# Small tables issued later, token diagonals and squares made sooner, in the start of a one-core transformer step

## The chip, the cores and the metric

The kernel runs on one core of a Trainium2 chip. The core has a matrix engine (TensorE, PE in the profile), three engines for elementwise work (VectorE or DVE, ScalarE or ACT, GpSimd or POOL), a fifth that only issues transfers here (SyncE, SP), and 16 DMA engines that all issuers share. The metric is the time of one execution on the device in microseconds. Three executions of the kernel before took 838.27, 839.02 and 839.62 us; the median is 839.02 us.

## The reference

One layer of a hybrid backbone is applied to 512 latent tokens and 128 context tokens of width 1024: an adaptive RMS norm, one input projection, two kinds of linear attention, an output projection, and a mixture of 32 experts. The change lies ahead of the input projection, so only this part matters:

```python
def rmsnorm(x, w):
    y = xf * lax.rsqrt(jnp.mean(xf * xf, axis=-1, keepdims=True) + EPS)
    return (y * w.astype(jnp.float32)).astype(x.dtype)

mod = (jax.nn.silu(cond) @ w_ada + b_ada)[:, None, :]      # w_ada: 1024 x 6144
sh1, sc1, g1, sh2, sc2, g2 = jnp.split(mod, 6, axis=-1)
h = rmsnorm(x, norm1_w) * (1 + sc1) + sh1
proj = h @ w_in                                            # w_in: 1024 x 3616
```

There are two conditioning vectors, one for the latent tokens and one for the context tokens. The gate biases, gate matrices, head norms and retention decays are small inputs that are used after `proj`.

## The kernel before, in words

The 640 tokens are five tiles of 128 rows (`X[:, t, :]`, 512 KB each). The input projection needs them with the channels on the partitions, so each tile is turned, and the turn also applies the root of the norm: for tile t, TensorE multiplies each of eight 128x128 pieces of X by a diagonal matrix `diag[t]` whose entries are the 128 roots of the tile's rows. Four turned pieces fill one bank of PSUM, so a tile fills two banks, called the half 0 and the half 1 of a turned tile (job `("xT", t, half)`, line 1574). ACT moves half 0 to `hT`, DVE moves half 1 (`turned_half`, lines 806 to 809 and 1039 to 1042). These moves are called evictions below.

A diagonal is made in a chain over three engines, each step on the one before: ACT sums the squares of the tile's rows (line 813), DVE turns the sum into a mean square (step `("ms0", t)`, helper line 1035), POOL takes the root with a power of -0.5 (step `("rs0", t)`, `root`, line 653), and DVE multiplies the identity by the roots (step `("diag", t)`, line 1057).

The modulation needs `w_ada`. Its columns for the shift (m = 0) and the scale (m = 1) come as eight loads of 1 MB, `("ada", m, i)`, each of which is used by one chunk of four matmuls (`chunk(m, i)`, line 1554). SP issues all weight loads through a ring of four slots (line 523): load n waits until load n-4 has been used. The chunks of m = 0 sum in a bank that DVE copies at line 1062, those of m = 1 in another, copied at line 1069. Both sums are then brought onto partitions by eight small matmuls (`("mT", m)`, line 1585). Only when `mT` 1 has been read (lines 1047 and 1072, step `mcol`) are the turned tokens scaled and shifted (lines 825 and 1080), and the first matmul of the input projection (line 1634) waits for the first of these.

The order of TensorE's work in this start is the list `START` (lines 114 and 115). Banks are given out in that order, seven in turn, and a matmul that starts a bank waits until its last content has been evicted. Each of the other engines runs its own list in program order; it waits in place for what it needs. ACT issues the loads of the conditioning vectors, of the constants and of the five token tiles; POOL issues the small tables.

The consumers of the small tables are these: the biases and the norm of line 629 and 630 feed the matmul at line 1566 (`bT`); the columns `gbias`, `nw` and `lg` (semaphore `s_cols`) are waited for by ACT ahead of line 828 and by DVE at line 1123; `wgate` (`s_gate`) by TensorE at line 1642; `brow` and `wrow` (`s_mrow`) much later, in the modulation rows after the attention scores.

Of the kernel before, what the change touches and what calls it, by code (L numbers as in the profile page):

```python
# [7 lines left out]
KC = D // P  # L8
# [97 lines left out]
def turn(t):  # L106
    return [("xT", t, half) for half in range(2)]


def chunk(m, i):  # L110
    return [("ada", m, i)]


START = chunk(0, 0) + chunk(0, 1) + chunk(0, 2) + chunk(0, 3) + [("bT",)] + turn(0) + chunk(1, 0) + turn(1) + [("mT", 0)]
START += turn(2) + chunk(1, 1) + turn(3) + chunk(1, 2) + turn(4) + chunk(1, 3) + [("mT", 1)]


def plan_loads():
# [61 lines left out]
def build(nc, inp, outs):  # L180
# [10 lines left out]
    with ExitStack() as ctx:  # L191
# [176 lines left out]
        def is_filled(eng, job):  # L368
            b, turn = where(job)
            eng.wait_ge(filled[b], turn + 1)  # L370
# [24 lines left out]
        dve_order = []  # L395
        for t in range(TILES):
            dve_order += [("ms0", t), ("diag", t)]
            if t == 2:
                dve_order += ["mcol0"]
        dve_order += ["mr1", "mcol"] + [("hT", k, part) for part in ("lat", "ctx") for k in range(0, KC, 2)]  # L400
        act_order = ["cS", "cS32"] + [("ss", t) for t in range(TILES)]
        act_order += [("hT", k, part) for part in ("lat", "ctx") for k in range(1, KC, 2)] + ["lg", "softplus"]
        pool_order = ["cS32"] + [("rs0", t) for t in range(TILES)]
# [216 lines left out]
        def _(pool):  # L620
            chain = [0]

            def link(ins):
                chain[0] += 1
                ins.then_inc(pool_chain, 1)
                pool.wait_ge(pool_chain, chain[0])

            pool_done(nc.gpsimd.memset(cS32, 0.0), "cS32")
            pool.dma_start(modr[0:2 * KC, :], b_ada[0, 0:2 * D].rearrange("(k p) -> k p", p=P)).then_inc(s_row, 16)
            pool.dma_start(modr[2 * KC:3 * KC, :], norm1_w[0].rearrange("(k p) -> k p", p=P)).then_inc(s_row, 16)  # L630
            with nc.allow_non_contiguous_dma(reason="small columns"):
                for d, v in enumerate((ggbf, ggbb)):
                    pool.dma_start(gbias[:, d, :], v[0].rearrange("(g p) -> p g", p=P)).then_inc(s_cols, 16)
                for d, v in enumerate((ret_norm_w, gla_norm_w)):
                    pool.dma_start(nw[:, 4 * d:4 * d + 4], v[0].rearrange("(h p) -> p h", p=P)).then_inc(s_cols, 16)
# [2 lines left out]
            link(nc.gpsimd.memset(wgate, 0.0))  # L638
            for d, v in enumerate((ggwf, ggwb)):
                pool.dma_start(wgate[RANK * d:RANK * (d + 1), d, :], v[0]).then_inc(s_gate, 16)  # L640
            link(nc.gpsimd.memset(power, -0.5))
            link(nc.gpsimd.memset(ones_c, 1.0))

            link(nc.gpsimd.memset(wrow, 1.0))
            for cond in range(2):
                r0 = cond * 32
                pool.dma_start(brow[r0:r0 + 32, :], b_ada[0, 2 * D:6 * D].rearrange("(c n) -> c n", n=P)).then_inc(s_mrow, 16)
                pool.dma_start(wrow[r0 + 16:r0 + 24, :], norm2_w[0].rearrange("(c n) -> c n", n=P)).then_inc(s_mrow, 16)

            def root(ap, key, rkey):  # L650

                dve.wait(pool, key)
                pool_done(nc.gpsimd.tensor_tensor(ap, ap, power[:, 0:ap.shape[1]], ALU.pow), rkey)  # L653

            for t in range(TILES):
                root(rstd[:, t:t + 1], ("ms0", t), ("rs0", t))


            is_filled(pool, ("xT", CTX, 1))
            for n, (dst, c0) in enumerate(((rel[0], R_RELF), (rel[1], R_RELB), (tft[0], R_TF), (tft[1], R_TB))):  # L660
                pool.dma_start(dst, rconsts[:, c0:c0 + dst.shape[1]]).then_inc(s_rc, 16)

            def level_exponents(n):

# [119 lines left out]
        def _(sc):  # L784
# [21 lines left out]
            def turned_half(t):  # L806
                job = ("xT", t, 0)
                is_filled(sc, job)
                drains(f(hT[:, 0:4, t * P:(t + 1) * P], bk(job)[:, :].rearrange("p (k t) -> p k t", k=4), ACT.Copy), job)

            for t in range(TILES):
                sc.wait_ge(s_x[t], 16)
                act.done(f(xn[:, t, :], X[:, t, :], ACT.Square, accum_out=ss[:, t:t + 1]), ("ss", t))
                if t:
                    turned_half(t - 1)
            turned_half(CTX)
            sc.dma_start(tail[:, 0:2048], consts[:, C_ROT:C_ONES]).then_inc(s_tail, 16)
            sc.dma_start(ones_s, consts[:, C_ONES:C_ONES + P]).then_inc(s_tail, 16)
            for t in range(TILES):
# [203 lines left out]
        def _(dv):  # L1023
# [27 lines left out]
            for t in range(TILES):  # L1051
                act.wait(dv, ("ss", t))
                dve.done(mean_square(rstd[:, t:t + 1], ss[:, t:t + 1], D), ("ms0", t))
                if t:
                    turned_half(t - 1)
                pool_s.wait(dv, ("rs0", t))
                dve.done(v.tensor_scalar(diag[t], ident[:, :], rstd[:, t:t + 1], None, ALU.mult), ("diag", t))
                if t == 1:
                    is_filled(dv, ("bT",))
                    drains(v.tensor_copy(bn.rearrange("p m k -> p (m k)"), bk(("bT",))[:, 0:3 * KC]), ("bT",))  # L1060
                    is_filled(dv, ("mr",))
                    drains(v.tensor_copy(first_mod_rows[0], bk(("mr",))[:, :]), ("mr",))
                if t == 2:
                    is_drained(dv, ("bT",))
                    modulation(0)
                    dve.done(v.memset(st3[:, 0:1], 0.0), "mcol0")
            turned_half(CTX)
            dv.wait_ge(scale_summed, 1)
            dve.done(v.tensor_copy(first_mod_rows[1], mod_ps[:, :]), "mr1")
            modulation(1)  # L1070
# [906 lines left out]
```

## Time and profile before

| what | value |
|---|---|
| median of three executions | 839.02 us (838.27 to 839.62) |
| the profiled execution | 835.24 us |
| its span | 833.5 us |
| TensorE busy | 723.8 us, 87% of the span |
| DVE, POOL, ACT busy | 392.8, 207.0, 155.6 us |
| mean granted clock of TensorE | 0.951 |

The span runs from the first instruction to the last; the 1.7 us around it belong to the execution but not to the trace. TensorE is busy in nearly every slice of the span, but not in the first 20 us, where its work waits for the first loads. The start that the change touches is the first 46 us: five turned tiles and eight chunks. All times below count from the start of the span.

### The profile page before, as it was taken

The page shows a single profiled execution, that of the slowest core. Times are in us where ns is not written, and L with a number is a line of the kernel's source. Part 1 is how long each engine was busy: PE and PEld are TensorE (multiplying, and loading weights), DVE is VectorE, ACT ScalarE, POOL GpSimd, SP SyncE. Part 2 cuts the span into 40 slices and gives each one's busy share as a digit, 9 for nine tenths or more (in the row PEclk, how much of TensorE's full clock was granted, in tenths as well). Part 3 has the DMA queues.
Part 4 walks back from the last instruction along what each step waited for, and adds up shares of the span by engine and source line. Part 5 has one row for each costly group of instructions (what it writes and reads, how often), then busy time and mean ns, then how long its engine had stood idle before and what let it go on. Part 6 is the DMA issues. An engine that isn't in the chain of part 4 may idle for free.

```text
span 833.5 us, 10843 instructions
## 1 busy us (share of the span) xinstructions
PE 723.8 (87%) x4297; PEld 466.6 (56%) x4297; DVE 392.8 (47%) x782; ACT 155.6 (19%) x257; POOL 207.0 (25%) x239
## 2 busy tenths in 40 slices
PE   2999995999999999999899999889999777778730
PEld 0655453558888556577688886445554433344410
DVE  0270499687576774755825334713223212211227
ACT  1331322012323215412201111111111001001002
POOL 5100044133333101112300000124444333322213
PEclk9999998899999999999999999989999999999975
DMA  9953403413333343335139417949999999999955
GB/s 301 367 196 110 149 1 104 149 52 100 102 102 101 103 151 113 127 117 145 49 142 399 193 77 275 382 144 362 384 370 387 397 384 392 397 385 389 389 199 240
DMA packets 74307, 186.02 MB, mean 223 GB/s; under 512 B 10012, under 2 KB 47044, under 8 KB 65296
## 3 DMA queue, kind: packets, MB, share of 16 engines
q1 hardware_dynamic: 62688, 159.94, 52.0%
q0 software_dynamic: 6144, 12.83, 4.8%
q10 hardware_dynamic: 5424, 12.55, 4.0%
q8 instruction: 35, 0.57, 0.3%
q14 instruction: 16, 0.13, 0.0%
HBM read 174.48 MB, written 17.10 MB: 230 GB/s over the span
## 4 chain that ended last, share of the span: by engine, by line
PE 61%; DMA 13%; DVE 11%; SPq 8%; issue 3%; ACT 2%; POOL 2%; DVEq 0%; POOLq 0%; ACTq 0%
PE bank L1634 18%; DMA weights_x_h<-in_expert_w_up 9%; PE bank L1851 7%; PE bank L1797 7%; PE bank L1624 4%; PE bank L1867 4%; SPq L527 3%; DVE qkv_gates_tables L1114 3%; SPq L526 3%; DMA weights_x_h<-in_w_ada 2%; PE bank L1753 2%; PE bank L1662 2%; SPq L530 2%; PE bank L1744 2%; PE bank L1696 2%
## 5 line engine op out<-in xcount | busy, mean ns | idle before, releaser
L1634 PE MATMUL bank<-weights_x_h 128*128 128x128 f32 (+3 forms) x672 | 189.0, 442 | 1.4 <-DVE weights_x_h L1080 1.4
L1634 PEld LDWEIGHTS bank<-weights_x_h 128*128 128x128 f32 (+1 forms) x672 | 102.9, 190 | 88.5 <-issue 86.5
L1851 PE MATMUL bank<-qkv_gates_tables,attention 128*64 128x256 f32 x480 | 60.0, 407 | 15.2 <-DMA qkv_gates_tables<-in_expert_w_up 14.3
L1449 DVE TENSOR_TENSOR attention<-attention,bank 128x128 f32<-128x128 f32 x32 | 9.2, 288 | 134.8 <-ACT attention L994 134.8
L1624 PE MATMUL bank<-weights_x_h 128*128 128x256 f32 x320 | 70.3, 380 | 0.0
L1624 PEld LDWEIGHTS bank<-weights_x_h 128*128 128x128 f32 x320 | 60.4, 190 | 9.3 <-DVE attention L1098 0.8
L1851 PE MATMUL bank<-weights_x_h,attention 128*64 128x256 f32 x416 | 50.9, 400 | 15.0 <-DMA weights_x_h<-in_expert_w_up 15.0
L1797 PE MATMUL bank<-weights_x_h 128*128 128x256 f32 x256 | 56.2, 380 | 0.0
L1851 PEld LDWEIGHTS bank<-qkv_gates_tables,attention 128*64 128x64 f32 x480 | 35.9, 146 | 34.9 <-DMA qkv_gates_tables<-in_expert_w_up 15.8
L653 POOL TENSOR_TENSOR small<-small 128x1 f32<-128x1 f32 (+1 forms) x20 | 15.7, 785 | 153.7 <-DVE small L1035 153.7
L1470 DVE SCALAR_TENSOR_TENSOR attention<-bank,slot_weights,qkv_gates_tables 128x512 f32<-128x512 f32 x32 | 24.0, 751 | 61.7 <-PE bank L1867 61.7
L1797 PEld LDWEIGHTS bank<-weights_x_h 128*128 128x128 f32 x256 | 48.4, 190 | 6.5
L1114 DVE SCALAR_TENSOR_TENSOR qkv_gates_tables<-weights_x_h,small,qkv_gates_tables 128x256 f32<-128x256 f32 x112 | 51.1, 531 | 0.0
L1851 PEld LDWEIGHTS bank<-weights_x_h,attention 128*64 128x64 f32 x416 | 30.2, 143 | 31.9 <-DMA weights_x_h<-in_expert_w_up 16.3
L1114 DVE SCALAR_TENSOR_TENSOR weights_x_h<-weights_x_h,small 128x256 f32<-128x256 f32 x112 | 48.0, 502 | 0.0
L994 ACT ACTIVATE attention<-bank 128x128 f32<-128x128 f32 x32 | 8.9, 278 | 202.6 <-PE bank L1851 197.4
L687 POOL TENSOR_TENSOR qkv_gates_tables<-qkv_gates_tables 128x512 f32<-128x512 f32 x8 | 15.1, 1893 | 112.9 <-ACT qkv_gates_tables L882 112.9
L747 POOL DMA_INDIRECT pick_rows<-attention,slot_rows_now x32 | 32.5, 1015 | 28.1 <-POOL slot_rows_now L744 28.1
L738 POOL DMA_INDIRECT attention<-hn_rows,slot_tokens_now x32 | 31.5, 986 | 28.0 <-POOL slot_tokens_now L733 24.6
L744 POOL COPY slot_rows_now<-slot_rows 128x1 int32<-128x1 int32 x32 | 22.5, 703 | 43.7 <-DVE attention L1470 43.7
L733 POOL COPY slot_tokens_now<-slot_tokens 64x1 int32<-64x1 int32 x32 | 5.8, 182 | 101.5 <-PE bank L1842 73.9
L1662 PE MATMUL bank<-attention 64*128 64x128 f32 x320 | 21.6, 289 | 8.5 <-DVE qkv_gates_tables L1155 8.5
(286 smaller groups left out, 1009.3 us busy)
## 6 DMA issues: line engine op xcount, KB each, us to landing
weights_x_h<-in_w_ada SPq DMA_DIRECT2D x24, 1024.0 KB, 6.9
qkv_gates_tables<-in_expert_w_gate SPq DMA_DIRECT2D x15, 1024.0 KB
qkv_gates_tables<-in_expert_w_up SPq DMA_DIRECT2D x15, 1024.0 KB
qkv_gates_tables<-in_expert_w_down SPq DMA_DIRECT2D x15, 1024.0 KB, 26.5
weights_x_h<-in_w_in SPq DMA_DIRECT2D x14, 1024.0 KB, 7.5
weights_x_h<-in_expert_w_gate SPq DMA_DIRECT2D x13, 1024.0 KB
weights_x_h<-in_expert_w_up SPq DMA_DIRECT2D x13, 1024.0 KB
weights_x_h<-in_expert_w_down SPq DMA_DIRECT2D x13, 1024.0 KB
```

The lines of the kernel that those rows point to most:

```text
L526: sp.dma_start(exb[b][:, 0:UNIT], ewg_v[bass.ds(e * P, P), :]).then_inc(s, 16)
L527: sp.dma_start(exb[b][:, UNIT:2 * UNIT], ewu_v[bass.ds(e * P, P), :]).then_inc(s, 16)
L738: pool.indirect_dma_start(xg[b], None, hn_dram[:, :], bass.IndirectOffsetOnAxis(ap=idxc[b][:, :].bitcast(U32), axis=0), bounds_check=T - 1 ...
L747: pool.indirect_dma_start(ys_dram[:, :], bass.IndirectOffsetOnAxis(ap=sidxc[n][:, :].bitcast(U32), axis=0), yb[n], None, bounds_check=2 * ...
L1114: ins = v.scalar_tensor_tensor(acc, w[:, k], cS[:, a, k:k + 1], acc, ALU.mult, ALU.add)
L1470: v.scalar_tensor_tensor(yb[n], bank[4 + n][:, :], weight, g2s[n], ALU.mult, ALU.mult).then_inc(y_ready, 1)
L1624: ins = mm(ps[:, 0:ITEM], hT[:, k, t * P:(t + 1) * P], wt[:, k, :], start=(k == 0), stop=(k == KC - 1))
L1634: ins = mm(ps[0:m, 0:hi - lo], wt[:, k, c * m:(c + 1) * m], hT[:, k, lo:hi], start=(k == 0), stop=(k == KC - 1))
L1662: ins = mm(halves[a][:, o:o + P], keys, lqk[pp, 0, g, tt], start=True, stop=True)
L1797: ins = mm(ps[:, 0:ITEM], hT[:, k, t * P:(t + 1) * P], wt[:, k, :], start=(k == 0), stop=(k == KC - 1))
L1851: ins = mm(bank[2 + n][j * SLOTS:(j + 1) * SLOTS, 0:2 * P], xte[n][:, k, :], exgu[b][:, :, k, j * P:(j + 1) * P], start=(k == 0), stop=(k ...
L1867: ins = mm(bank[4 + n][half * SLOTS:(half + 1) * SLOTS, :], hidT[n][:, j, :], exd[b][:, j, half * 512:(half + 1) * 512], start=(j == 0), s ...
```

## The change

Four edits are made, all ahead of the input projection.

1. POOL issues 12 small transfers later. The six of lines 633 to 637, the gate matrices (line 640) and their memset, the memset of `wrow` and the four transfers of lines 647 and 648 come behind the five roots; the last four also come behind the four of line 661. The two memsets that the roots need stay ahead.
2. ACT sums the squares of tiles 0 to 3 before its first eviction, and those of tile 4 behind one eviction.
3. DVE makes the diagonals of tiles 0, 1 and 2 before its first eviction, and those of tiles 3 and 4 behind one and two evictions. The copies of the biases and of the first sums stand behind the diagonal of tile 2, `mcol0` behind that of tile 4.
4. TensorE turns tile 4 directly behind tile 3, and the chunks (1, 2) and (1, 3) follow together.

```diff
-START += turn(2) + chunk(1, 1) + turn(3) + chunk(1, 2) + turn(4) + chunk(1, 3) + [("mT", 1)]
+START += turn(2) + chunk(1, 1) + turn(3) + turn(4) + chunk(1, 2) + chunk(1, 3) + [("mT", 1)]
...
             pool.dma_start(modr[2 * KC:3 * KC, :], norm1_w[0].rearrange("(k p) -> k p", p=P)).then_inc(s_row, 16)
+            link(nc.gpsimd.memset(power, -0.5))
+            link(nc.gpsimd.memset(ones_c, 1.0))
+            ...
+            for t in range(TILES):
+                root(rstd[:, t:t + 1], ("ms0", t), ("rs0", t))
+
             with nc.allow_non_contiguous_dma(reason="small columns"):
...
-            link(nc.gpsimd.memset(power, -0.5))
-            link(nc.gpsimd.memset(ones_c, 1.0))
-
+            is_filled(pool, ("xT", CTX, 1))
+            for n, (dst, c0) in enumerate(((rel[0], R_RELF), (rel[1], R_RELB), (tft[0], R_TF), (tft[1], R_TB))):
+                pool.dma_start(dst, rconsts[:, c0:c0 + dst.shape[1]]).then_inc(s_rc, 16)
             link(nc.gpsimd.memset(wrow, 1.0))
...
                 act.done(f(xn[:, t, :], X[:, t, :], ACT.Square, accum_out=ss[:, t:t + 1]), ("ss", t))
-                if t:
-                    turned_half(t - 1)
-            turned_half(CTX)
+                if t >= 3:
+                    turned_half(t - 3)
+            for t in range(TILES - 3, TILES):
+                turned_half(t)
...
                 dve.done(mean_square(rstd[:, t:t + 1], ss[:, t:t + 1], D), ("ms0", t))
-                if t:
-                    turned_half(t - 1)
                 pool_s.wait(dv, ("rs0", t))
                 dve.done(v.tensor_scalar(diag[t], ident[:, :], rstd[:, t:t + 1], None, ALU.mult), ("diag", t))
-                if t == 1:
+                if t == 2:
+                    is_filled(dv, ("mr",))
+                    drains(v.tensor_copy(first_mod_rows[0], bk(("mr",))[:, :]), ("mr",))
                     is_filled(dv, ("bT",))
                     drains(v.tensor_copy(bn.rearrange("p m k -> p (m k)"), bk(("bT",))[:, 0:3 * KC]), ("bT",))
-                    is_filled(dv, ("mr",))
-                    drains(v.tensor_copy(first_mod_rows[0], bk(("mr",))[:, :]), ("mr",))
-                if t == 2:
-                    is_drained(dv, ("bT",))
-                    modulation(0)
-                    dve.done(v.memset(st3[:, 0:1], 0.0), "mcol0")
-            turned_half(CTX)
+                    turned_half(0)
+                if t == 3:
+                    turned_half(1)
+            is_drained(dv, ("bT",))
+            modulation(0)
+            dve.done(v.memset(st3[:, 0:1], 0.0), "mcol0")
+            for t in range(2, TILES):
+                turned_half(t)
```

On POOL's queue, from the second small load on, before the change: the transfers are the rows with DMA, the roots are the row with `x5`.

```order
L630 DMA small<-in_norm1_w 8x128
L633 DMA small<-in_gla_gate_b_fwd 128x2x1
L633 DMA small<-in_gla_gate_b_bwd 128x2x1
L635 DMA small<-in_ret_norm_w 128x4x1
L635 DMA small<-in_gla_norm_w 128x4x1
L637 DMA small<-in_ret_decay_fwd 128x4
L637 DMA small<-in_ret_decay_bwd 128x4
L638 MEMSET qkv_gates_tables 32x512
L640 DMA qkv_gates_tables<-in_gla_gate_w_fwd 16x256
L640 DMA qkv_gates_tables<-in_gla_gate_w_bwd 16x256
L641 MEMSET small 128x5
L642 MEMSET small 128x32
```

The same place of POOL's queue after the change:

```order
L628 DMA small<-in_norm1_w 8x128
L629 MEMSET small 128x5
L630 MEMSET small 128x32
L635 ISA
L635 TENSOR_TENSOR small<-small 128x1 x5
L642 DMA small<-in_gla_gate_b_fwd 128x2x1
L642 DMA small<-in_gla_gate_b_bwd 128x2x1
L644 DMA small<-in_ret_norm_w 128x4x1
```

The transfers of the columns and gates moved from a place where POOL waits for nothing to one behind the fifth root.

DVE's start before the change, from the first mean square on; `bank3`, `bank5` and `bank1` hold the half 1 of tiles 0, 1 and 2, `attention<-ident,small` is a diagonal:

```order
L1035 TENSOR_SCALAR small<-small 128x1
L1057 TENSOR_SCALAR attention<-ident,small 128x128
L1035 TENSOR_SCALAR small<-small 128x1
L1042 COPY weights_x_h<-bank3 128x4x128
L1057 TENSOR_SCALAR attention<-ident,small 128x128
L1060 COPY small<-bank1 128x24
L1062 COPY attention<-bank0 128x512
L1035 TENSOR_SCALAR small<-small 128x1
L1042 COPY weights_x_h<-bank5 128x4x128
L1057 TENSOR_SCALAR attention<-ident,small 128x128
```

The same place after the change:

```order
L1033 TENSOR_SCALAR small<-small 128x1
L1053 TENSOR_SCALAR attention<-ident,small 128x128
L1033 TENSOR_SCALAR small<-small 128x1
L1053 TENSOR_SCALAR attention<-ident,small 128x128
L1033 TENSOR_SCALAR small<-small 128x1
L1053 TENSOR_SCALAR attention<-ident,small 128x128
L1056 COPY attention<-bank0 128x512
L1058 COPY small<-bank1 128x24
L1040 COPY weights_x_h<-bank3 128x4x128
L1033 TENSOR_SCALAR small<-small 128x1
L1053 TENSOR_SCALAR attention<-ident,small 128x128
L1040 COPY weights_x_h<-bank5 128x4x128
```

The eviction of tile 0's half 1 moved behind the diagonals of tiles 1 and 2.

## Rows read from the trace of the kernel before

**Rows 1.** The profile's page: the span, and 40 slices of TensorE.

```profile
span 833.5 us, 10843 instructions
PE   2999995999999999999899999889999777778730
```

**Rows 2.** The chain of waits, from 0 us: start, us, what held the chain.

```profile
2.31 19.14 DMA weights_x_h<-in_w_ada
21.49 1.93 PE bank L1554 x8
...
23.65 3.71 PE bank L1574 x16
...
32.34 1.89 PE bank L1574 x16
34.23 0.99 PE bank L1554 x8
35.22 2.03 PE bank L1574 x16
...
41.35 0.70 DVE attention L1069
...
42.10 1.96 PE bank L1585 x16
...
45.49 34.54 PE bank L1634 x112
```

**Rows 3.** DMA queues in 7 to 12 us: packets, MB, share of 16 engines.

```profile
q1 hardware_dynamic: 249, 0.95, 52.9%
q0 software_dynamic: 165, 0.01, 33.3%
q10 hardware_dynamic: 253, 0.11, 8.2%
```

**Rows 4.** DMA queues in 3 to 7 us, that of POOL.

```profile
q0 software_dynamic: 59, 0.01, 1.8%
```

**Rows 5.** DMA queues in 12 to 17 us, those of SP and POOL.

```profile
q1 hardware_dynamic: 265, 1.02, 50.7%
q0 software_dynamic: 220, 0.07, 9.1%
```

**Rows 6.** Timeline of POOL: start, us, what, idle time before.

```profile
2.68 0.80 POOL L633 DMA_DIRECT2D small<-in_gla_gate_b_fwd  x1
...
11.04 0.52 POOL L648 DMA_DIRECT2D small<-in_norm_w  x1
...
35.29 0.55 POOL L653 TENSOR_TENSOR small<-small 128x1 f32<-128x1 f32 x1 [1.97 <-DVE small L1035]
40.59 1.17 POOL L661 DMA_DIRECT2D qkv_gates_tables<-in_rconsts  x2 [4.75 <-PE bank L1574]
```

**Rows 7.** Timeline of DVE: the diagonals of tiles 3 and 4.

```profile
34.87 0.28 DVE L1057 TENSOR_SCALAR attention<-ident,small 128x128 f32<-128x128 f32 x1
...
37.90 0.28 DVE L1057 TENSOR_SCALAR attention<-ident,small 128x128 f32<-128x128 f32 x1
```

**Rows 8.** Timeline of ACT: squares of tile 2, the decays, the projection's first eviction.

```profile
26.19 1.05 ACT L813 ACTIVATE qkv_gates_tables<-weights_x_h 128x1024 f32<-128x1024 f32 x1
...
49.06 1.28 ACT L828 ACT_TABLE_LOAD   x1
...
54.10 0.60 ACT L867 ACTIVATE attention<-bank 128x512 f32<-128x512 f32 x1 [3.29 <-PE bank L1634]
```

**Rows 9.** Windows: PE, PEld, DVE, ACT, POOL busy, PEclk, DMA share, GB/s.

```profile
45.00:48.50 3.50, 3.01 (x4) 1.49 (x5) 3.50 (x11) 3.50 (x7) 0.00 (x0) 0.51 1.00 395
140.60:150.90 10.30, 5.33 (x27) 3.84 (x28) 10.16 (x20) 2.82 (x2) 0.05 (x1) 0.50 0.52 173
```

**Rows 10.** DMA issues, 0 to 60 us: size of each, median us to landing.

```profile
small<-in_ret_decay_bwd POOLq DMA_DIRECT2D x1, 2.0 KB, 8.1
```

**Rows 11.** DMA issues, 28.5 to 29 us.

```profile
weights_x_h<-in_w_in SPq DMA_DIRECT2D x1, 1024.0 KB, 9.0
```

More of the change, by code:

```diff
@@ L397, in build @@
             dve_order += [("ms0", t), ("diag", t)]
-            if t == 2:
-                dve_order += ["mcol0"]
-        dve_order += ["mr1", "mcol"] + [("hT", k, part) for part in ("lat", "ctx") for k in range(0, KC, 2)]
+        dve_order += ["mcol0", "mr1", "mcol"] + [("hT", k, part) for part in ("lat", "ctx") for k in range(0, KC, 2)]
         act_order = ["cS", "cS32"] + [("ss", t) for t in range(TILES)]
@@ L630, in _, with root @@
             pool.dma_start(modr[2 * KC:3 * KC, :], norm1_w[0].rearrange("(k p) -> k p", p=P)).then_inc(s_row, 16)
+            link(nc.gpsimd.memset(power, -0.5))
+            link(nc.gpsimd.memset(ones_c, 1.0))
+            def root(ap, key, rkey):
+                dve.wait(pool, key)
+                pool_done(nc.gpsimd.tensor_tensor(ap, ap, power[:, 0:ap.shape[1]], ALU.pow), rkey)
+            for t in range(TILES):
+                root(rstd[:, t:t + 1], ("ms0", t), ("rs0", t))
             with nc.allow_non_contiguous_dma(reason="small columns"):
@@ L648, in _ @@
                 pool.dma_start(wrow[r0 + 16:r0 + 24, :], norm2_w[0].rearrange("(c n) -> c n", n=P)).then_inc(s_mrow, 16)
[L650 to L661, printed above, removed]
             def level_exponents(n):
@@ L1053, in _ @@
                 dve.done(mean_square(rstd[:, t:t + 1], ss[:, t:t + 1], D), ("ms0", t))
-                if t:
-                    turned_half(t - 1)
                 pool_s.wait(dv, ("rs0", t))
                 dve.done(v.tensor_scalar(diag[t], ident[:, :], rstd[:, t:t + 1], None, ALU.mult), ("diag", t))
-                if t == 1:
+                if t == 2:
+                    is_filled(dv, ("mr",))
+                    drains(v.tensor_copy(first_mod_rows[0], bk(("mr",))[:, :]), ("mr",))
                     is_filled(dv, ("bT",))
                     drains(v.tensor_copy(bn.rearrange("p m k -> p (m k)"), bk(("bT",))[:, 0:3 * KC]), ("bT",))
-                    is_filled(dv, ("mr",))
-                    drains(v.tensor_copy(first_mod_rows[0], bk(("mr",))[:, :]), ("mr",))
-                if t == 2:
-                    is_drained(dv, ("bT",))
-                    modulation(0)
-                    dve.done(v.memset(st3[:, 0:1], 0.0), "mcol0")
-            turned_half(CTX)
+                    turned_half(0)
[6 more added lines that the diff above has]
+                turned_half(t)
             dv.wait_ge(scale_summed, 1)
```

## The prediction, made before the changed kernel was run

> **What bounds the kernel now.** I read the page's slices first. TensorE is busy in nearly all of them except the first: the two leading digits are 2 and 9, so the first 20.8 us hold the only long stretch near the change in which the bounding engine idles [rows 1]. Second I read the chain of waits through the start [rows 2]. Up to 21.45 us it is one transfer, 19.14 us of waiting for `w_ada`: that is the landing of the last chunk (0, 3) of the shift. From 21.49 us to 41.33 us the chain never leaves TensorE: chunks and turned tiles stand without a gap. Then come the copy of the scale sums (41.35), the eight small matmuls (42.10) and, at 45.49 us, the projection, which is TensorE's again. So two things can shorten this start: an earlier landing, or less work or fewer lost moments on TensorE between 21.5 and 45.5 us. The evictions and the diagonals are not on the chain.
>
> Third I asked what the DMA engines did while TensorE waited. From 7 to 12 us POOL's queue took 33.3% of the 16 engines' time, for 0.01 MB, while `w_ada` on SP's queue had 52.9% [rows 3]. From 3 to 7 us POOL's had 1.8% [rows 4], from 12 to 17 us 9.1% [rows 5]. These are the small tables, which POOL issued from 2.68 to 11.56 us [rows 6].
>
> The last view is the timeline of the evicting engines. ACT squared tile 2 only at 26.19 us, behind an eviction [rows 8]. DVE finished the diagonal of tile 3 at 35.15 us, 0.07 us ahead of the turn that reads it (35.22), and that of tile 4 at 38.18 us [rows 7, 2]. So the diagonals came just in time.
>
> **The small tables, the large term.** POOL's queue took 4 x 0.018 = 0.07 us, 5 x 0.333 = 1.67 us and 5 x 0.091 = 0.46 us of all 16 engines' time before 17 us [rows 3 to 5], in sum 2.19 us. Two small loads stay where they are; they can be no more than the 0.07 us of the first stretch. The moved twelve therefore cost 2.1 us of the engines ahead of the chain's landing.
>
> How much of it reaches the landing depends on who takes the freed time. In 7 to 12 us SP's queue moved 249 packets and ACT's 253: the two take turns, packet by packet [rows 3]. ACT's are short ones (0.11 MB), its constants; when they are done its token tiles begin, and SP's share stays at a half, 50.7% [rows 5]. If taking turns goes on, both queues reach each point of this sequence 1.67 us sooner, and the 0.46 us behind it likewise: 2.1 us, all of it. Below that the bound is 0, if ACT's queue takes all. Above, SP's queue alone takes the 33.3%: 52.9% would become 86.2%, and 0.95 MB would become 1.55 MB; at the 1.02 MB per 5 us of the next stretch these 0.60 MB are 2.9 us, with the 0.46 us 3.4 us. I take 2.1, since the packet counts are the nearest rows. The 5.6% of 7 to 12 us in which no queue had the engines (0.28 us) I leave out of the sum and in the range.
>
> The Trainium skill (DMA: Bandwidth & Descriptors, Issuing engines are not separate DMA queues) says that transfers issued from different engines run on the same 16 DMA engines and interleave; the packet counts of 7 to 12 us agree. The same page (Bandwidth, Measured) gives 0.68 us of engine time for a transfer of 4 KB; twelve would be 8.2 us, an estimate from the page, and the sum would be some 6 us larger by it. The share measured here, 2.1 us, goes against that and is used.
>
> **The diagonals and squares, a small term.** The chain has no wait for a diagonal, so no wait goes. What could go is the time in which the weights of a turn's first matmul are not loaded ahead, because the diagonal is not there yet. The turn of tile 2, whose diagonal was early, took 1.89 us; that of tile 3, whose diagonal came 0.07 us ahead, 2.03 us [rows 2]. Two such turns give 2 x 0.14 = 0.28 us; the difference may be chance. Bounds 0 and 0.3, I take 0.2.
>
> **Tile 4 directly behind tile 3.** The work on TensorE is the same, so the sum gets nothing. The chunks (1, 2) and (1, 3) now stand last; both were landed long before. The third slot's next load leaves one turn later, 2.0 us, but is read only by DVE's row sums behind the projection's start. The last evictions have two chunks (some 2.0 us) in front of the scale copy where they had one (1.04 us, the same kind as the 0.99 at 34.23). DVE's and ACT's last evictions stay off the chain.
>
> **What is issued later, and its cover.** The new POOL queue starts the twelve transfers after the fifth root. That root waits for DVE's fifth mean square, which stands behind the eviction of tile 1. Counting from the end of tile 1's turn, which was about two turns and eight small matmuls ahead of 34.23, I estimate the root's end at 30 us. The old issue of these twelve took 11.56 - 2.68 = 8.9 us [rows 6], with all columns in its first half; so the columns leave by 35 us and, at the longest landing seen (8.1 us) [rows 10], are there by 43 us. ACT needs them for the decays at 50.3 us (the end of the table load at 49.06), now some 2.3 us sooner, 48 us [rows 8]. The cover is 5 us; behind it ACT's next eviction was at 54.10 us, so another 4 us cost TensorE nothing. The gate matrices are read far later, behind two more items of the projection.
>
> The same packets now take turns with the loads for the last chunks and the projection's first weights. Those were issued at 28.75 us (the start of the issue lies in the window of [rows 11]) and landed in 9.0 us, at 37.8 us, against a use at 45.49 us: 7.7 us of cover, of which 2.1 us go to the tables. The diagonal of the last tile was ready before its turn although it stood behind three evictions [rows 7]; now it stands behind two, and its turn comes one chunk sooner. DVE has it by about 31 us, the turn begins at about 35 us.
>
> **Sum.** 2.1 + 0.2 + 0 = 2.3 us off the start. From 45.49 us the projection is TensorE's, its loads are released by its own matmuls, so the shift goes through to the end. The profiled execution had 835.24 us; 835.24 - 2.3 = 832.9 us. The three timed ones were slower, 839.02 us in the median, 3.8 us above; I take the difference over to them: 839.02 - 2.3 = 836.7 us.
>
> **Rivals.** (a) The landing does not move, or half of it: ACT's queue takes the freed time, or the slowest of 16 engines, which sets a landing, is not the one that the tables loaded. For it: 0.01 MB in 33.3% of the time is odd traffic that can lie unevenly. Against it: the turns are even, and 5.6% were idle. Time: between no gain and 1.2 us, 838.4 us.
>
> (b) TensorE's clock answers the shift, to the good. In the start it runs at the lower of its two levels (1.2 GHz): eight records of a chunk take 1.93 us at 21.49 us and 0.99 us at 34.23 us [rows 2]. Behind the pause at 44 us the granted clock is 0.51, nearly all at 1.2 GHz, for 3.5 us with TensorE busy for 3.01 [rows 9]; this costs 1.5 us. If the moved pause is not answered with a fall, 836.7 - 1.5 = 835.2 us. For it: nothing in the trace fixes the fall at that place. Against it: the pause keeps its length.
>
> (c) The other side: the fall lasts as long as the one from 140.6 us, where the clock stood at 1.2 GHz for 10.3 us [rows 9]. The place is the projection's first matmuls. A fall of 10.3 us costs about (10.3 - 0.5) / 2 = 4.9 us in place of 1.5; with the 2.3 us gained that is +1.1 us, 840.1 us. It decides when the clock stays low for more than about 8 us, 3.5 + 2 x 2.3. Against it: that long fall came with long stretches in which TensorE did nothing, here it is fully busy from the first projection matmul on.
>
> (d) The tables come too late. The Trainium skill (SBUF — State Buffer, SBUF: two separate sides) says that a transfer issued from GpSimd can starve, because its descriptors cannot be written while VectorE runs in a two-port mode. No run here shows it: POOL's two issues beside DVE's copies at 40.59 us took 1.17 us for two, 0.58 each, against 0.80 for one at 2.68 us [rows 6]. It begins to cost when the columns land 9 us later than I reckon, at 52 us, and each further microsecond costs at most one: at 4 us of it, 840.7 us.
>
> **How the numbers follow.** Forecast (1.7 to 3 us gained) 0.50, larger gain by (b) or the upper bound of the landing 0.14, (a) 0.26, (c) 0.06, (d) 0.04. What a measurement of this kernel can tell from no change is about 0.2%, 1.7 us. Faster by more than that: the first two, 0.64. Within: (a) and most of (c), 0.30. Slower by more: 0.06, from (d) and the worst of (c). The likeliest case alone spans 836.0 to 837.3 us. For 8 in 10 I go down to 834.6, which takes in (b) and the 3.4 us bound (839.02 - 3.4 - 0.3 = 835.3), and up to 839.6, which takes in (a) and the spread of the three executions.
>
> **What the profile of the changed kernel would show.** Right: POOL's queue has nothing but its first two loads before 17 us; the chain leaves the `w_ada` transfer at about 19.3 us in place of 21.45; the copy of the scale sums begins at about 39.0 us and the projection at 43.1. The turns of tiles 3 and 4 take 1.9 us each; all five diagonals are done by about 31 us. ACT reaches the decays without waiting. The forecast is wrong if the landing stays above 20.8 us, if TensorE waits for a bank or for a diagonal between landing and projection, or if the projection starts sooner but the span does not shrink with it.

## The result and the profile after

The changed kernel is faster, by about twice what was forecast.

| | before | changed |
|---|---|---|
| median | 839.02 us (833.56 to 839.67, 5 runs) | 833.67 us (831.34 to 834.89, 5 runs) |
| ratio of the runs, 95% interval | | 0.9946 (0.9920 to 0.9972) |
| profiled execution | 835.24 us | 833.67 us |
| its span | 833.5 us | 831.9 us |

The ratio is a gain of 4.5 us, with an interval of 2.3 to 6.7 us. The two medians are 5.35 us apart. The two profiled spans are only 1.6 us apart, and why is worked out below.

The first lines to read are the span and TensorE's slices. The first two digits went from 2 and 9 to 3 and 8.

```profile
span 831.9 us, 10844 instructions
PE   3899996999999999999899999889999777788730
```

The chain of waits of the changed kernel through its start (start, us, what held the chain) answers to [rows 2]:

```profile
2.31 15.23 DMA weights_x_h<-in_w_ada
17.54 0.04 issue
17.58 1.94 PE bank L1553 x8
...
19.75 3.21 PE bank L1573 x16
22.95 0.99 PE bank L1553 x8
...
30.50 3.77 PE bank L1573 x32
34.27 1.90 PE bank L1553 x16
...
36.19 0.70 DVE attention L1068
```

The last chunk of the shift lands at 17.54 us, before at 21.45. The projection starts at 40.32 us, before at 45.49. The 5.17 us between them are the landing (3.91), the turn of tile 0 (3.71 to 3.21, 0.50), the chunk behind it (1.31 to 0.99, 0.32), the turns of tiles 3 and 4 (4.06 to 3.77, 0.29) and the last two chunks (2.04 to 1.90, 0.14).

DMA queues of the changed kernel from 7 to 12 us (packets, MB, share of 16 engines), against [rows 3]:

```profile
q1 hardware_dynamic: 389, 1.47, 74.3%
q10 hardware_dynamic: 400, 0.53, 29.9%
q0 software_dynamic: 10, 0.00, 0.1%
```

POOL's queue is all but gone from this stretch. SP's and ACT's queues still take turns, 389 packets against 400, but now at about 79 a microsecond each instead of 50.

### The profile page after: what moved, and what is told of

Read it like the earlier page. It is cut to its first block, busy times and chain, and to the rows that moved or that the text cites. A ratio compares the mean times of both kernels' runs of the same rounds, so it can differ in the third digit from the quotient of the medians.

```text
span 831.9 us, 10844 instructions
## 1 busy us (share of the span) xinstructions
PE 725.4 (87%) x4297; PEld 467.4 (56%) x4297; DVE 393.4 (47%) x782; ACT 155.7 (19%) x257; POOL 206.9 (25%) x239
## 4 chain that ended last, share of the span: by engine, by line
PE 61%; DMA 12%; DVE 11%; SPq 8%; issue 3%; ACT 2%; POOL 2%; DVEq 0%; POOLq 0%; ACTq 0%
PE bank L1633 18%; DMA weights_x_h<-in_expert_w_up 10%; PE bank L1850 7%; PE bank L1796 7%; PE bank L1623 4%; PE bank L1866 4%; SPq L525 3%; DVE qkv_gates_tables L1113 3%; SPq L524 3%; SPq L528 2%; DMA weights_x_h<-in_w_ada 2%; PE bank L1661 2%; PE bank L1752 2%; PE bank L1743 2%; PE bank L1695 2%
## 5 line engine op out<-in xcount | busy, mean ns | idle before, releaser
L1866 PE MATMUL bank<-qkv_gates_tables,attention 128*64 128x512 f32 x120 | 29.0, 604 | 0.0
```

The costliest lines, as they stand in the source:

```text
L1866: ins = mm(bank[4 + n][half * SLOTS:(half + 1) * SLOTS, :], hidT[n][:, j, :], exd[b][:, j, half * 512:(half + 1) * 512], start=(j == 0), s ...
```

## Experiments

Each edit is shown against the kernel named. Landing means the landing of the last shift chunk, 0.04 us ahead of the start of the chunk that uses it. Ratios are to the kernel before, run on the same chip.

### 1. The tables alone

```diff
 # the kernel before, with POOL's part of the changed kernel
+            for t in range(TILES):
+                root(rstd[:, t:t + 1], ("ms0", t), ("rs0", t))
...
+            with nc.allow_non_contiguous_dma(reason="small columns"):
+                ...
```

> The kernel before with edit 1 alone: the twelve small transfers behind the roots, while squares, diagonals, evictions and TensorE's order stay as they were. Theory A (the whole large term is the small tables in the DMA engines): the last w_ada chunk of the shift lands at 17.5 us as in the changed kernel (21.45 before), the projection starts at about 41 us, 4 us sooner than before, and the time is 3.5 to 4.5 us under the kernel before, ratio 0.995 to 0.996. Rival B (the new order of squares and diagonals brings most of what the forecast missed): landing at about 19.3 us, projection at about 43.3 us, ratio 0.997 to 0.998.

Ratio 0.9955 (0.9933 to 0.9977), median 834.62 us over 12 runs. The row of the timeline of TensorE (start, us, what, idle before) that shows the landing:

```profile
17.89 1.93 PE L1553 MATMUL bank<-weights_x_h,small 128*32 128x512 f32 x8 [3.88 <-DMA weights_x_h<-in_w_ada]
```

Landing at 17.85 us, 0.3 us from the changed kernel's, and the projection started at 41.22 us, 4.27 us sooner than before. Theory A holds: edit 1 carries nearly the whole gain.

### 2. The order alone

```diff
 # the changed kernel, with POOL's part of the kernel before
-            for t in range(TILES):
-                root(rstd[:, t:t + 1], ("ms0", t), ("rs0", t))
             with nc.allow_non_contiguous_dma(reason="small columns"):
...
+            for t in range(TILES):
+                root(rstd[:, t:t + 1], ("ms0", t), ("rs0", t))
```

> The changed kernel with the small tables issued early again, at their old place: edits 2 to 4 alone. Theory A: landing at 21.4 us, the turns of tiles 3 and 4 take 3.8 us together in place of 4.06, the projection starts at 45.1 us, 0.3 to 0.4 us sooner, ratio 0.9995 or so, not to be told from 1. Rival B: landing at 21.4 us, but a projection at 43.5 us or sooner, ratio 0.998.

Ratio 0.9994 (0.9974 to 1.0014). In TensorE's timeline the landing stays, and the turns of tiles 3 and 4 are one group:

```profile
21.44 1.94 PE L1554 MATMUL bank<-weights_x_h,small 128*32 128x512 f32 x8 [2.92 <-DMA weights_x_h<-in_w_ada]
...
33.95 3.84 PE L1574 MATMUL bank<-attention,weights_x_h 128*128 128x128 f32 x32
37.71 1.92 PE L1554 MATMUL bank<-weights_x_h,small 128*32 128x512 f32 x16
```

Its projection started at 44.06 us, 1 us sooner than expected, because the turn of tile 0 took 2.72 us instead of 3.78: its instructions reached their full speed sooner in this profile. In the times the order brings nothing that can be told from no change.

### 3 and 4. Which tables

```diff
 # 3: the changed kernel
             pool.dma_start(modr[2 * KC:3 * KC, :], ...)
+            link(nc.gpsimd.memset(wgate, 0.0))
+            for d, v in enumerate((ggwf, ggwb)): ...
+            ... (wrow, brow)
 # 4: the changed kernel
             pool.dma_start(modr[2 * KC:3 * KC, :], ...)
+            ... (gbias, nw, lg: the six columns)
```

> The changed kernel, but of the twelve small transfers only the six of the columns (gate biases, head norms, decays: 128 partitions each) are late; the two gate matrices and the four modulation rows (16, 16, 32, 8, 32 and 8 partitions) are issued at the start, right behind the first two small loads. Theory C (the tables cost what their queue took of all 16 engines, and the columns, most of the packets, are most of it): landing at about 18 to 18.5 us, ratio to before about 0.996. Rival D (a landing waits for the slowest of the 16 engines, and the transfers of few partitions, which lie on few engines, are what holds it): landing at about 20 us, ratio about 0.998.

> The mirror of the last: the six column transfers early, the gate matrices and the modulation rows late. Theory C: landing at about 20.5 us, ratio about 0.999. Rival D: landing at about 18.5 us, ratio about 0.996. If both this and its mirror land at about 19.5 us, the cost goes with the number of transfers and not with their kind.

With only the columns late (3) the ratio is 0.9945 (0.9923 to 0.9968), with only the columns early (4) 0.9990 (0.9968 to 1.0013). TensorE's timeline of 3 and then of 4:

```profile
19.07 1.94 PE L1553 MATMUL bank<-weights_x_h,small 128*32 128x512 f32 x8 [3.02 <-DMA weights_x_h<-in_w_ada]
```

```profile
21.07 1.94 PE L1553 MATMUL bank<-weights_x_h,small 128*32 128x512 f32 x8 [3.16 <-DMA weights_x_h<-in_w_ada]
```

The columns are the cost. The transfers of few partitions are not, so that half of rival D falls; its other half, that a landing waits for the slowest of the 16 engines, is taken up below. The landing of 3 looks 1.5 us late, though its time is as good as the changed kernel's. Experiment 7 explains it.

### 5. The four transfers of 4-byte elements

```diff
 # the changed kernel
+            with nc.allow_non_contiguous_dma(reason="small columns"):
+                ... (gbias and nw only; lg stays late)
             link(nc.gpsimd.memset(power, -0.5))
```

> The changed kernel, but of the twelve small transfers the four of gate biases and head norms, which are copied element by element (4 bytes each, 1536 elements in all), are early; the decays, a row of 16 bytes to each partition, stay late with the rest. Theory H (the cost goes with the 4-byte elements): landing at 20.5 to 21 us, as with all six columns early (21.03). Rival I (the cost goes with the number of transfers of 128 partitions): four sixths of the 3.5 us, landing at 19.9 us.

Ratio 0.9980 (0.9958 to 1.0002), landing at 21.26 us. Two rows of TensorE's timeline:

```profile
7.76 1.94 PE L1553 MATMUL bank<-weights_x_h,small 128*32 128x512 f32 x8 [7.76 <-ACT small L801]
...
21.30 1.94 PE L1553 MATMUL bank<-weights_x_h,small 128*32 128x512 f32 x8 [3.02 <-DMA weights_x_h<-in_w_ada]
```

Both forecasts were made from landings of the first of two patterns of the start (experiment 7); this profile has the second, in which the changed kernel lands 1.3 us later. Shifted by that, theory H asks for 21.8 to 22.3 us and rival I for 21.2 us, so the landing is rival I's. Against the changed kernel in the same pattern (18.80 us) the four transfers cost 2.5 us of 4.3. By the ratio they give back 0.34 of the 0.54 per cent. The two decay transfers therefore carry the rest, although their pieces are rows of 16 bytes and not single elements. The queues say the same. POOL's row from 2 us to the landing, here and then with all six columns early (experiment 4):

```profile
q0 software_dynamic: 192, 0.02, 5.0%
```

```profile
q0 software_dynamic: 256, 0.02, 9.7%
```

Of 19.26 and 19.03 us this is 0.96 and 1.85 us (4 has the first pattern): the two decay transfers added some 0.9 us, as much as the four with 4-byte elements.

### 6. The same data as rows

```diff
 # the changed kernel
+            for n, (r0, v) in enumerate(((0, ggbf), (2, ggbb), (4, ret_norm_w), (8, gla_norm_w))):
+                nr = 2 if n < 2 else 4
+                pool.dma_start(onorm[0][r0:r0 + nr, 0, :], v[0].rearrange("(g p) -> g p", p=P)).then_inc(s_spare, 16)
             link(nc.gpsimd.memset(power, -0.5))
```

> The changed kernel, with four transfers added at the start that bring the gate biases and the head norms as rows: 12 rows of 512 bytes in place of 1536 elements of 4 bytes, same data, into memory that nobody reads; all twelve small transfers stay late. Theory H (the 4-byte elements hold single DMA engines up, and a landing waits for the slowest engine): landing as in the changed kernel, 17.5 to 18.8 us, time equal to the changed kernel, ratio to before 0.9945. Rival I (any small transfers of POOL's at that place cost the landing some 0.6 us each): landing at 20 us, ratio 0.997.

Ratio 0.9957 (0.9936 to 0.9977). DMA queues from 7 to 12 us, and TensorE's timeline:

```profile
q1 hardware_dynamic: 392, 1.49, 74.7%
q10 hardware_dynamic: 397, 0.50, 28.4%
q0 software_dynamic: 128, 0.01, 1.7%
```

```profile
17.61 1.94 PE L1558 MATMUL bank<-weights_x_h,small 128*32 128x512 f32 x8 [3.18 <-DMA weights_x_h<-in_w_ada]
```

The landing is that of the changed kernel, 17.57 us. Rival I would have had it at 20 us and falls: the 6 KB of the four element transfers cost nothing as 12 rows of 512 bytes at the same place of the same queue. The decays were not tried in another form. POOL's queue moved 128 packets in these 5 us with 1.7% of the engines' time, where the kernel before, with all its tables, had 165 packets with 33.3% [rows 3].

### 7. Both kernels profiled once more

No edit.

> The changed kernel once more, for a second profile. If the landing of the last shift chunk is a property of the program it comes at 17.5 us again; where TensorE's first chunk starts at 7.7 us instead of 8.5 (as in half of the profiles so far), it comes about 1.2 us later, at 18.7 us.

> The kernel before once more, for a second profile. Landing at 21.45 us again, or about 22.6 us where the first chunk starts at 7.7 us; either way 3.9 us behind the changed kernel in the same pattern.

One execution each: 835.69 us changed, 840.43 us before. TensorE's timeline of the changed kernel, then of the kernel before:

```profile
7.62 3.25 PE L1553 MATMUL bank<-weights_x_h,small 128*32 128x512 f32 x16 [7.62 <-ACT small L801]
...
18.84 1.94 PE L1553 MATMUL bank<-weights_x_h,small 128*32 128x512 f32 x8 [3.02 <-DMA weights_x_h<-in_w_ada]
```

```profile
7.76 1.94 PE L1554 MATMUL bank<-weights_x_h,small 128*32 128x512 f32 x8 [7.76 <-ACT small L804]
...
23.14 1.94 PE L1554 MATMUL bank<-weights_x_h,small 128*32 128x512 f32 x8 [2.91 <-DMA weights_x_h<-in_w_ada]
```

The start has two patterns. In one TensorE's first chunk starts at 8.4 to 9.3 us (the two first profiles, and those of 1, 2, 4, 6, 9 and 11), in the other at 7.6 to 7.8 us (3, 5, 8, 10 and these two). In the second pattern ACT's queue is further ahead early on (0.04 MB from 3 to 7 us in the changed kernel's second profile, 0.01 MB in its first), and the landing comes 1.3 us (changed, 17.54 to 18.80) or 1.7 us (before, 21.45 to 23.10) later. Within a pattern the change is worth 3.9 and 4.3 us. At these later landings SP's queue had moved 4.73 MB (before) and 4.44 MB (changed), which is used below. What decides between the patterns is not known. The pattern also mends experiment 3: its 19.03 us belongs beside 18.80, so gates and modulation rows cost 0.2 us.

### 8. The columns twice

```diff
 # the kernel before, behind its six column transfers
+                for d, v in enumerate((ggbf, ggbb)):
+                    pool.dma_start(spare[:, 2 * d:2 * d + 2], v[0].rearrange("(g p) -> p g", p=P)).then_inc(s_spare, 16)
+                ... (nw and lg likewise)
```

> The kernel before with the six column transfers issued twice at the start, the second time into memory that nobody reads. Theory C (every such transfer costs engine time and delays the chain): the landing moves from 21.45 to 24.5 or 25 us (3.5 us for the columns, as the pair of mirrored experiments showed with 21.03 against 17.54), time 3 to 4 us over the kernel before, ratio 1.004. Rival G (the cost is one of having POOL's queue active at all beside the others, not of each transfer): landing at 22 us, ratio 1.001.

Ratio 1.0034 (1.0012 to 1.0056), 2.9 us slower: nearer to theory C. The profile says less. Its landing is at 23.57 us, in the second pattern, where the kernel before has 23.10, so by the landing rival G (0.6 us later) is the nearer. The engines reached their parts of this load 1.43 us later on average, 22.43 against 21.00 us, but the last of them was only 1.14 us behind that mean, where it had been 2.10 us behind (how these are read stands in the next section). What a second set costs is therefore seen in the times, and only in part in this one profile, whose execution (835.99 us) was the fastest of the ten.

### 9. Tile 4 turned last

```diff
 # the changed kernel
-START += turn(2) + chunk(1, 1) + turn(3) + turn(4) + chunk(1, 2) + chunk(1, 3) + [("mT", 1)]
+START += turn(2) + chunk(1, 1) + turn(3) + chunk(1, 2) + chunk(1, 3) + turn(4) + [("mT", 1)]
...
-            for t in range(2, TILES):
+            for t in range(2, CTX):
                 turned_half(t)
             dv.wait_ge(scale_summed, 1)
             dve.done(v.tensor_copy(first_mod_rows[1], mod_ps[:, :]), "mr1")
+            turned_half(CTX)
```

> The changed kernel with tile 4 turned last: TensorE does the chunks (1, 2) and (1, 3) ahead of tile 4's turn, and DVE copies the scale sums ahead of that tile's eviction, so the copy (0.7 us) stands beside the turn instead of in a pause. Theory: TensorE runs without a gap from the landing to the end of mT 1, the projection starts 0.75 us sooner than in the changed kernel (39.6 us at the same landing), and the time is 0.7 us less, ratio to before about 0.9935. If the shorter pause also keeps the granted clock up, 1.5 to 3 us less, ratio 0.990 to 0.992. Rival: the fall of the clock sits in the second pause (1.4 us) and the eight tiny matmuls and stays, with the same length.

Ratio 0.9937 (0.9916 to 0.9959), median 832.08 us. The end of the start in TensorE's timeline:

```profile
32.07 1.92 PE L1554 MATMUL bank<-weights_x_h,small 128*32 128x512 f32 x16
33.92 2.05 PE L1574 MATMUL bank<-attention,weights_x_h 128*128 128x128 f32 x16
35.81 1.84 PE L1585 MATMUL bank<-small,attention 128*128 128x2 f32 x16
39.10 13.45 PE L1634 MATMUL bank<-weights_x_h 128*128 128x512 f32 x36 [1.44 <-DVE weights_x_h L1080]
```

The pause ahead of the eight small matmuls is gone, and the projection starts at 39.10 us at the same landing, 1.22 us sooner than in the changed kernel. Of these 0.34 us were there already at the chunk behind tile 0's turn (22.54 against 22.88 us, the clock rose sooner); the other 0.88 us are the edit's, 0.81 us of them the pause. The median is 1.6 us lower; the intervals of the two ratios overlap, so a gain over the changed kernel is not shown. The clock fell all the same, with the same length, as the rival had it:

```profile
38.00:44.90 6.90, 5.80 (x7) 2.52 (x8) 6.57 (x19) 6.17 (x11) 2.77 (x6) 0.51 1.05 394
```

### 10 and 11. Idle matmuls against the fall of the clock

```diff
 # 10: experiment 9; 11: the changed kernel
                     fills(ins, job)
+                    if m == 1:
+                        keep_warm(2)
```

> The last kernel with two idle matmuls (128x512, result read by nobody) behind mT 1, in the time in which DVE makes the scale columns (about 1.3 us). Theory E (what the changed kernel loses behind 40 us is the granted clock, 6.8 us at 1.2 GHz from 39.3 us, and it falls because TensorE is idle there): no stretch at 1.2 GHz at the projection's start, the first eight matmuls of the projection take 4.7 us or less in place of some 7 us, and the time is 1.5 to 3 us under e5. Rival F: the clock falls all the same, or the two matmuls end after the columns are ready and delay the projection by up to 0.6 us; time equal to e5 or 0.5 us above.

> The changed kernel with two idle matmuls (128x512) behind mT 1 and nothing else. Theory E (TensorE's idle time there brings the clock down, and that costs the changed kernel 1.5 to 3 us): no stretch at 1.2 GHz between 38 and 46 us, ratio to before 0.991 to 0.993. Rival F: the stretch stays or the gain is within the 0.2 us by which the idle matmuls delay the projection; ratio 0.9945.

Experiment 10 (on top of 9): ratio 0.9930 (0.9907 to 0.9953), median 832.05 us. Experiment 11: ratio 0.9949 (0.9931 to 0.9967). The windows of the changed kernel, of 10 and of 11 (us; PE, PEld, DVE, ACT and POOL busy; granted clock; DMA share; GB/s):

```profile
39.30:46.20 6.90, 5.88 (x7) 2.53 (x8) 3.88 (x13) 6.17 (x11) 0.00 (x0) 0.51 1.04 369
```

```profile
38.40:46.00 7.60, 7.60 (x20) 3.51 (x20) 7.05 (x21) 6.17 (x11) 3.27 (x7) 1.00 1.04 397
```

```profile
38.50:42.00 3.50, 3.50 (x6) 1.49 (x7) 3.01 (x10) 2.87 (x5) 0.49 (x1) 0.53 1.02 405
```

In the profile of 10 TensorE keeps the higher level, 2.4 GHz, through the start of the projection. In that of 11 it still falls, for 3.4 us, and the idle matmuls themselves run in it: they took 3.50 us and held the projection back to 41.74 us. In the times neither is told from its partner without them (0.9930 against 0.9937, 0.9949 against 0.9946). So theory E had its higher clock in one profile of two and its gain of 1.5 to 3 us in neither; rival F stands. That the idle matmuls shorten the fall is not shown either: without them it lasted 3.4 us in the first profile of the kernel before and in those of 4 and 5, and 6.8 us in the others. Experiment 10 had the lowest median of all kernels by a hair; that it beats 9 is not shown.

## Why the prediction was wrong

**The step that failed: "how much of it reaches the landing".** The sum let the landing move by the time that POOL's queue took of all 16 engines, as if that time lay evenly on them; the landing waited for the slowest one. The amount was right. From 2 us to the landing POOL's queue had 11.3% of 19.45 us before, 2.20 us, against a forecast of 2.19. But the landing moved by 3.9 us, where 2.1 was taken and 3.4 was the upper bound. The queues from 2 us to the landing, of the kernel before and then of the changed one:

```profile
q1 hardware_dynamic: 1184, 4.59, 62.7%
q10 hardware_dynamic: 1035, 1.82, 25.1%
q0 software_dynamic: 448, 0.10, 11.3%
```

```profile
q1 hardware_dynamic: 1122, 4.33, 71.3%
q10 hardware_dynamic: 977, 1.64, 28.4%
q0 software_dynamic: 64, 0.01, 0.4%
```

Multiplied by 19.45 and 15.54 us, the difference of 3.91 us is: POOL's queue 2.20 - 0.06 = 2.14 us, SP's 12.20 - 11.08 = 1.12 us, ACT's 4.88 - 4.41 = 0.47 us, and 0.2 us with no queue. Of SP's 1.12 us, 0.69 us are 0.26 MB more at 2.66 us a MB; the rest is that its bytes took longer, 2.66 against 2.56 us a MB. The four chunks are 4.19 MB. At their landing SP's queue had moved 4.59 MB before and 4.33 MB after: 0.40 MB of later loads had overtaken them, against 0.14 MB. In the second profiles it was 0.54 against 0.25 MB, and with the rows early (experiment 6) 0.15 MB. The reading is that some of the 16 engines had finished their part and gone on to the next loads while others had not, and a landing waits for the last. (The Trainium skill, DMA: Bandwidth & Descriptors, Queues, rings and completion order, says that each engine takes the descriptors of a queue in order; with that, later loads can only have been begun by engines that had begun all of their part.)

The trace shows this directly. A load's completion is counted in 16 steps, and the trace has the time of each. First step, mean of the 16 and last step of the four shift chunks, in us:

| chunk | before: first, mean, last | changed: first, mean, last |
|---|---|---|
| (0, 0) | 5.49, 5.74, 6.09 | 5.31, 5.75, 6.04 |
| (0, 1) | 9.06, 9.97, 11.32 | 8.13, 8.62, 8.96 |
| (0, 2) | 13.80, 14.95, 16.48 | 11.65, 12.24, 12.59 |
| (0, 3) | 18.96, 20.02, 21.45 | 16.61, 17.20, 17.54 |

Before, the steps of a load drew apart to over 2 us just while the tables moved (7 to 12 us) and stayed apart; in the changed kernel they stay within 1 us. Of the 3.91 us at the last chunk, 2.82 us are the mean and 1.09 us are the last step's distance from it (1.43 against 0.34 us). The mean's part is near POOL's 2.14 us with the slower bytes (0.43) and the time with no queue (0.2), 2.8 us in sum. The last step's part is near the two terms that are left, 0.69 and 0.47 us, which is what SP's and ACT's queues moved while the landing lagged. In the second profiles the two parts are 2.94 and 1.37 us, and the steps spread over 4.08 us before and 1.50 us in the changed kernel. With all columns early (4) the steps spread over 2.57 us, with the rows early (6) over 0.82 us. The byte counts say the same: with the element transfers early SP's queue had moved 4.56 MB at the landing in 2 and in 5, and 4.60 MB in 4. Which engines were late is not known: neither a packet nor a step of the trace names its engine.

What holds an engine up is seen in single packets. Of POOL's 165 packets from 7 to 12 us before, 82 have 4 bytes and took 0.008 us each. Nearly all of the queue's 33.3% is in 80 packets of 64 or 128 bytes, made of the 4-byte elements and the 16-byte decays: 0.32 us each on average, from 0.015 to 1.22 us. SP's packets of 4096 bytes took 0.18 us on average. So such a packet cost more than one of 4096 bytes on average, and very unequally, which fits that the engines came apart; engine by engine it is not shown. A row of 512 bytes took 0.027 us (experiment 6). The Trainium skill (DMA: Bandwidth & Descriptors, Rules for kernel authors) says that a strided last dimension becomes one descriptor per element and should be rearranged. The trace shows packets and not descriptors; the advice agrees with experiments 5 and 6: 2.5 us of landing for the elements (21.26 against 18.80 us, second pattern), nothing for the rows (17.57 against 17.54 us, first pattern). The advice does not cover the decays, whose pieces are rows of 16 bytes. The Trainium skill (DMA: Bandwidth & Descriptors, Bandwidth, Measured) has 0.68 us for a transfer of 4 KB. The prediction's estimate from it, 8.2 us for twelve, was too much: POOL's queue took 2.20 us of the engines, and the landing moved by 3.9 us.

**The small term.** The forecast had 0.2 us for diagonals and nothing for the order of tile 4. The profile shows 0.29 us in the turns of tiles 3 and 4 and 0.14 us in the chunks that now follow each other, 0.43 us in sum. The size is about right, the mechanism mostly not. In experiment 9 the diagonals are as early, but the turns of tiles 3 and 4 stand apart, each behind a chunk. Its chain has for them:

```profile
30.16 1.98 PE bank L1574 x16
33.99 1.98 PE bank L1574 x16
```

Against 2.03 us each before, an early diagonal is worth 0.05 us, 0.1 us for both. The other 0.19 us of the turns and the 0.14 us of the chunks come with turns and chunks that follow their own kind, to which the prediction gave nothing. Its comparison of 2.03 with 1.89 us was of unlike places: the turn of tile 2 follows the small matmuls, not a chunk. Alone all this cannot be told from no change (experiment 2).

**The clock, rival (b) and (c).** Rival (b), a pause without a fall, did not happen in the changed kernel. Instead the rise came sooner in the turn of tile 0, which gives 0.82 us of the 5.17. This is read from the length of the instructions: the granted clock of the changed kernel is 0.50 up to 21.4 us and 1.00 from 23.4 us on, but for the kernel before it stands at 1.00 already at 21.5 us, where eight records of a chunk still took 1.93 us. Behind the pause the stretch at 1.2 GHz was 6.8 us long instead of 3.4 [rows 9], which is rival (c) in small, about 1.4 us of the lead: at the next group of the projection, 78.65 against 82.38 us, the lead is 3.73 us. The change is not shown to lengthen it, since the kernel before has a long one in its second profile:

```profile
46.10:53.10 7.00, 6.22 (x8) 2.63 (x9) 6.91 (x19) 6.05 (x11) 0.00 (x0) 0.51 1.01 379
```

From 90.5 us the changed kernel had another stretch of 6.8 us, where the kernel before had one of 3.4 us from 96.2 us:

```profile
90.50:97.40 6.90, 6.90 (x12) 3.14 (x11) 2.44 (x7) 2.90 (x2) 0.00 (x0) 0.51 0.27 88
```

It holds up 14 matmuls on the chain (5.63 us against 4.35), and DVE's scans start at 105.71 us against 108.17, a lead of 2.46 us. The later stages carry between 2.3 and 4.0 us up to the experts. There, where the chain waits for `in_expert_w_up`, the last long waits bring it from 2.4 to 1.5 us. This is how 5.17 us became 1.6 us in this pair of spans. The second profiles, 835.69 and 840.43 us, are 4.7 us apart with leads of 4.30 us at the landing and 5.08 us at the projection's start. The prediction had named as a sign of being wrong that the projection starts sooner and the span does not shrink with it. The first pair of profiles shows that sign and the second does not. The clock took or gave 0.8 to 1.4 us at a time in these profiles; the forecast was right that it does not decide.

**The cover.** Right: ACT reached the decays at 43.91 us for its table load without a wait, and the column tables were issued from 27.30 to 31.45 us, against an estimate of 30 to 35 us. The first projection weights were issued at 24.01 us and landed in 12.4 us, at 36.4 us, for a use at 40.32. The cover fell from 7.7 to 3.9 us, more than the 2.1 us reckoned. One new wait appeared, on DVE, off the chain. The prediction had named this load, which leaves one turn later, but no wait for it:

```profile
45.26 0.62 DVE L1110 TENSOR_SCALAR qkv_gates_tables<-weights_x_h,small 128x256 f32<-128x256 f32 x2 [2.70 <-DMA weights_x_h<-in_w_ada]
```

It cost nothing that the chain shows: from 40.32 to 78.07 us the chain stays with TensorE's projection.

**Rivals (a) and (d).** (a) had the right observation and the wrong sign: tables that lie unevenly on the engines raise what their removal brings. (d) did not happen: the columns' issues took 0.58 to 0.80 us each, as before. The prediction's 0.58 against 0.80 us compared unlike transfers: each kind took the same time early and late.

**Range and chances.** What came is the case of a larger gain, to which the prediction gave 0.14. The 833.67 us lie below the range, whose lower end was 834.6. That end was set from the 3.4 us bound and not from the clock and the bound together, 839.02 - 3.4 - 1.5 - 0.3 = 833.8 us, and the bound itself was too small, since it left out the slowest engine.

## What to carry to other kernels

When a transfer of many large loads is on the chain, look for a queue that takes a share of the DMA engines out of proportion to its bytes; small tables that are copied in pieces of 4 or 16 bytes belong behind the loads that the chain waits for; those of 4-byte elements can also be brought as rows, which cost nothing here. The share gives a lower estimate of what their removal brings, since a landing waits for the slowest of 16 engines; compare the bytes that the queue has moved at the landing with the bytes that had to land. Moving evictions and diagonals that are not on the chain brought nothing that could be measured alone.

## What the runs showed of the hardware that was not expected

- A packet of 64 or 128 bytes that is made of pieces of 4 or 16 bytes can take longer than one of 4096 bytes: 0.32 against 0.18 us on average from 7 to 12 us in the kernel before, and up to 1.22 us. A row of 512 bytes took 0.027 us.
- With such packets ahead of it a load lands raggedly: the 16 steps of its completion spread over 2.49 us before, over 0.93 us in the changed kernel and over 0.82 us with the same elements as rows.
- The same program starts in one of two patterns, with TensorE's first chunk at 7.6 to 7.8 or at 8.4 to 9.3 us, and the fourth chunk's landing 1.3 to 1.7 us later when it starts at 7.6 to 7.8.
- The stretch at 1.2 GHz behind the same pause lasted 3.4 us in one profile of the kernel before and 6.8 us in the other; with idle matmuls it was absent once and lasted 3.4 us once.
